# Dense products that read and write backwards, with the high and low parts of a weight side by side

## What is computed

```python
h = rms_norm(x, g_attn_pre[l]) * (1.0 + scale_a[:, None]) + shift_a[:, None]
proj = h @ w_in[l]
...
ff = (jax.nn.silu(h @ w_gate[l]) * (h @ w_up[l])) @ w_down[l]
```

## Time and profile before

| | |
|---|---|
| median of 3 executions | 2589.59 us (2586.76 to 2590.08) |
| the profiled execution | 2586.09 us, of it 2584.3 us span from first to last instruction |
| mean granted clock of TensorE | 0.979 |
| PE busy | 2479.3 us, 96% |
| weight loads (PEld) busy | 2348.3 us, 91% |
| DVE busy | 1439.8 us, 56% |
| ACT busy | 1032.9 us, 40% |
| read from HBM | 498.04 MB, 194 GB/s over the span |

### The profile page before, as it was taken

How to read it: one execution, slowest core, us unless ns; L and a number is a source line. 1 busy time by engine, 2 the same in 40 slices (tenths; PEclk the granted TensorE clock), 3 DMA queues, 4 the chain that set the end, 5 groups by cost and what they waited for, 6 DMA issues and landing times.

```text
span 2584.3 us, 47889 instructions
## 1 busy us (share of the span) xinstructions
PE 2479.3 (96%) x20022; PEld 2348.3 (91%) x20022; DVE 1439.8 (56%) x1926; ACT 1032.9 (40%) x1332; POOL 290.8 (11%) x372
## 2 busy tenths in 40 slices
PE   6999988989999999999989998998999999999999
PEld 4999857979999999999979997878999999999999
DVE  3687657966764444443455554755655555554443
ACT  3533244344333434333334445443444444443333
POOL 5000122410100000011113002113000000000000
PEclk8999989989999999999989999999999999999999
DMA  9887865977785555555544442314455555555553
GB/s 345 290 289 267 292 211 173 334 274 244 249 291 192 186 187 184 184 180 181 189 135 150 148 153 66 115 66 131 148 179 188 181 182 178 179 182 181 190 181 130
DMA packets 263862, 504.24 MB, mean 195 GB/s; under 512 B 17152, under 2 KB 26283, under 8 KB 263467
## 3 DMA queue, kind: packets, MB, share of 16 engines
q1 hardware_dynamic: 257899, 494.97, 57.0%
q10 hardware_dynamic: 5840, 7.52, 0.9%
HBM read 498.04 MB, written 2.10 MB: 194 GB/s over the span
## 4 chain that ended last, share of the span: by engine, by line
PE 80%; DVE 8%; ACT 4%; issue 4%; DMA 2%; SPq 1%; POOL 1%; DVEq 0%; ACTq 0%; POOLq 0%
PE bank L2110 24%; PE bank L2112 24%; PE bank L2111 24%; ACT w_hi L935 3%; DVE w_lo L1458 3%; PE bank L2145 2%; DMA raw<-in_w_in 1%; DVE tmp L1592 1%; DVE ada_acc L1486 1%; DMA staged<-in_w_ada 1%; SPq L646 1%; PE bank L2254 1%; SPq L739 1%; PE bank L2455 0%; ACT x_hi L1046 0%
## 5 line engine op out<-in xcount | busy, mean ns | idle before, releaser
L1458 DVE TENSOR_TENSOR w_lo<-raw,w_hi 128x2048 fp32r<-128x2048 f32 (+3 forms) x386 | 863.5, 2237 | 942.2 <-ACT w_hi L935 941.7
L2110 PE MATMUL bank<-x_hi,w_hi 128*128 128x256 f32 (+2 forms) x4608 | 1317.5, 286 | 35.6 <-DVE w_lo L1458 19.1
L2112 PE MATMUL bank<-x_hi,w_lo 128*128 128x256 f32 (+2 forms) x4608 | 1307.6, 284 | 0.0
L2111 PE MATMUL bank<-x_lo,w_hi 128*128 128x256 f32 (+2 forms) x4608 | 1301.2, 282 | 0.0
L935 ACT ACTIVATE w_hi<-raw 128x2048 fp32r<-128x2048 f32 (+3 forms) x386 | 718.7, 1862 | 1032.8 <-PE bank L2112 905.8
L2110 PEld LDWEIGHTS bank<-x_hi,w_hi 128*128 128x128 f32 x4608 | 873.0, 189 | 71.9 <-issue 40.7
L2111 PEld LDWEIGHTS bank<-x_lo,w_hi 128*128 128x128 f32 x4608 | 873.1, 189 | 1.2 <-issue 1.2
L2112 PEld LDWEIGHTS bank<-x_hi,w_lo 128*128 128x128 f32 x4608 | 872.2, 189 | 0.0
L2112 PE MATMUL bank<-hid_hi,w_lo 128*128 128x256 f32 x1408 | 397.0, 282 | 0.0
L2110 PE MATMUL bank<-hid_hi,w_hi 128*128 128x256 f32 x1408 | 394.1, 280 | 2.8 <-DVE w_lo L1458 1.5
L2111 PE MATMUL bank<-hid_lo,w_hi 128*128 128x256 f32 x1408 | 394.3, 280 | 0.0
(11 more groups left out here) (332 smaller groups left out, 1462.6 us busy)
## 6 DMA issues: line engine op xcount, KB each, us to landing
raw<-in_w_gate SPq DMA_DIRECT2D x88, 1024.0 KB, 5.2
raw<-in_w_up SPq DMA_DIRECT2D x88, 1024.0 KB, 5.2
raw<-in_w_ada SPq DMA_DIRECT2D x72, 1024.0 KB, 6.7
raw<-in_w_in SPq DMA_DIRECT2D x68, 1024.0 KB, 5.7
raw<-in_w_down SPq DMA_DIRECT2D x64, 1024.0 KB, 5.0
raw<-in_w_down SPq DMA_DIRECT2D x32, 768.0 KB, 4.3
beside<-in_w_ada SPq DMA_DIRECT2D x16, 1024.0 KB, 7.5
raw<-in_w_o SPq DMA_DIRECT2D x16, 1024.0 KB, 6.7
```

Of the source, the lines that this page charges most:

```text
L1458: dve.tensor_tensor(w_lo[ps][:, 0:width], raw[slot][:, 0:width], w_hi[ps][:, 0:width], ALU.subtract).then_inc(raw_free[slot], 1)
L2110: pe.matmul(out, wh[:, k, c], hi(k0 + k), start=a0, stop=False)
L2111: pe.matmul(out, wh[:, k, c], lo(k0 + k), start=False, stop=False)
L2112: ins = pe.matmul(out, wl_[:, k, c], hi(k0 + k), start=False, stop=z)
```

## The change

Two edits are made together.

The first is in `dense`: the token operand of each of the three matmuls and the PSUM output are given with the step -1 along the columns. The first column that PE reads is the last one of the row, and it is written to the last column of the output range. Each output column still receives the product of its own token column; results stand where they stood. Weights are still read from the first column to the last.

The second is in the layout of the split weights. In place of four tiles of 2048 columns there are two tiles `w_both` of 2048 by 2 numbers. The high part of a weight is the first 4 bytes of 8, its low part the other 4. The names `w_hi` and `w_lo` stay, as views whose columns lie 8 bytes apart. So ACT writes (L935) with a step of 8 bytes, DVE reads the high part and writes the low part (L1458) with a step of 8 bytes, and the weight loads of all dense matmuls read with that step. The four tiles take the same bytes in all, and everything behind them keeps its address. ACT's two sums of squares at the start (L981), which use `w_hi` as a place for output that nothing reads, write with that step too.

```diff
-        w_hi = [place(f"w_hi{i}", [P, UK * COLS], F32R) for i in range(SPLIT)]
-        w_lo = [place(f"w_lo{i}", [P, UK * COLS], F32R) for i in range(SPLIT)]
+        w_both = [place(f"w_both{i}", [P, UK * COLS, 2], F32R) for i in range(SPLIT)]
+        w_hi, w_lo = ([w[:, :, part] for w in w_both] for part in range(2))
...
-                        out = (banks(m) if banks else bank[base + m])[0:r, 0:n]
+                        out = (banks(m) if banks else bank[base + m])[0:r, 0:n][:, ::-1]
...
-                            pe.matmul(out, wh[:, k, c], hi(k0 + k), start=a0, stop=False)
-                            pe.matmul(out, wh[:, k, c], lo(k0 + k), start=False, stop=False)
-                            ins = pe.matmul(out, wl_[:, k, c], hi(k0 + k), start=False, stop=z)
+                            pe.matmul(out, wh[:, k, c], hi(k0 + k)[:, ::-1], start=a0, stop=False)
+                            pe.matmul(out, wh[:, k, c], lo(k0 + k)[:, ::-1], start=False, stop=False)
+                            ins = pe.matmul(out, wl_[:, k, c], hi(k0 + k)[:, ::-1], start=False, stop=z)
```

## The result

The changed kernel takes 2612.01 us (median of 4 executions, 2607.97 to 2615.33), the kernel before 2588.18 us (4 executions, 2582.34 to 2590.08): 1.0095 times as long, 95% interval 1.0081 to 1.0110, or 24 to 25 us more. The forecast was 2520 us, some 70 us less. The profiled execution took 2615.33 us, at the same mean clock of 0.979.

A forecast was written before the change was run, and what follows sets the result against it. PE's dense matmul steps were taken as the bound. Gains of 79 us, counted as 69 (63% in full, the rest at two thirds), took 2586.1 to 2517; the median's 3.5 us more gave about 2520, range 2470 to 2650.

The forecast's parts named there:

- The gain from streams that keep their distance: Dense matmuls: token reads and weight loads both cover 1024 bytes, so steps fall to 0.113 us with 256 columns; 79 us.
- The floor of 0.112: Lowest step for a dense matmul with 256 columns, in us, read from 128-column weight loads beside one-column matmuls.
- The weight loads with a step of 8 bytes: Dense matmuls' loads of 128 numbers: 6 ns of room, any price over 0.05 ns per number shows; taken as nothing.
- The rival "a few ns": PE's streams: new addresses meet more often, the mean step rises by 3 ns, 54 us, 2640 us; chance 0.10.
- a way to fail: Forecast fails if weight loads have their own rate for stepped reads, with only 6 ns to spare.
- ACT's stepped write: ACT's 2048 numbers per unit, 8 bytes apart: nothing to 0.77 ns per number (1.58 us); taken as nothing.
- the split was to become the bound: Splitting the weights outlasts its slack, from 0.54 ns per number if one engine pays; 2645 to 2985 us, chance 0.15.
- hidden up to the slack: Weight split: extra ACT and DVE time is hidden up to 1.10 us per unit; each us beyond costs half a us.
- DVE's price of nothing: DVE's 8-byte streams in the split: nothing to 1.58 us per unit; taken as nothing.
- Rival 1: Dense matmuls: the 10 to 12 ns are a fixed price of changing weights; 2585 to 2595 us, chance 0.12.
- The 64-column row: Profile row cited against the gain: matmuls with loads of 64 columns look the same as with 128, 300 ns mean.
- a case in which DVE pays for the step and PE gains: DVE pays 0.77 ns per number in the split while PE gains 4 ns a matmul; about 2645 us.

## Why the prediction was wrong

**The gain from streams that keep their distance: the step that failed first.** The sum gives it 79 us, counted as 69, of the 92 us between 2520 and 2612, and it rested on all steps falling to 0.113 us. They did not fall: with both edits the mean is 0.1186 us on `x_hi` and 0.1178 on `hid`, against 0.1173 and 0.1178 before. The direction gives 17 us back where the loads are stepped and takes 3 where they are adjacent, so against the kernel before there is no gain at all. The steps did become even, as expected, but not by the two edits together: backward reads alone do it (0.115 to 0.121 on `hid`, in place of 0.112 to 0.125), with the mean there unchanged and on `x_hi` 0.6 ns higher. Taking the unevenness away took no time away, and the short steps were no evidence of room. The floor of 0.112 was read from loads beside matmuls of one column; single steps with 256 columns come down to it, but no mean comes near. What the remaining 10 ns are made of stays open.

**The weight loads with a step of 8 bytes: taken as nothing.** "Any price over 0.05 ns per number shows at once", it said, and this held. A load of 128 numbers takes 8 ns more, 0.06 ns per number, and the matmul step rises by 0.1193 - 0.1168 = 2.5 ns in the window of the run with stepped loads. That is +31 us alone; with what the backward reads give back, 14 us are left of it in the changed kernel. The rival "a few ns" was the right one, with 3 ns and 54 us for its case and a chance of 0.10, and the end of the prediction names this price as a way to fail.

**ACT's stepped write: mis-sized.** Taken as nothing, it is 0.12 ns per number, 0.24 us per unit, far under the 0.54 from which the split was to become the bound. Yet it costs some 10 us: the rule "hidden up to the slack" was read at one unit, and fails at the places where PE already waits for the split. Rows 4 showed them, 20.6 us of idle time. The trace has 27 such waits; 27 x 0.24 = 6.5 us would have been a fair first estimate, and PE's waits for the split grew by 6.9 us. DVE's price of nothing was right. The Trainium skill's "Vector Engine (DVE) Microarchitecture Reference", section 5.2, which asks for two adjacent words beginning on an 8-byte boundary, does not hold for this step: 2304 ns against 2302, where the estimate from its table was 1.9 us more. The lines of 16 bytes with two hits in each, in the Trainium skill's "SBUF — State Buffer", section "Door 1", fit DVE (nothing at 8 bytes) and roughly the loads (8 ns at 8 bytes, 141 ns at 16), but not ACT's write (237 ns at 8 bytes).

**Rival 1's point that averages lie close** was half right. The 64-column row that spoke for a fixed price compares modelled durations; by start-to-start times in the whole trace the two are close as well, 0.1246 us with 64 columns loaded and 0.1252 with 128, both with 272 moving. But the price is not fixed: on `hid` the mean is 0.1203 us with stepped loads and forward columns, and 0.1200 without the gaps of 64 bytes. The kernel before sits at the best of the three placements tried.

**The range.** That 2612 lies within 2470 to 2650 is luck. The upper end was drawn for a case in which DVE pays for the step and PE gains, and neither happened.

**What was argued only:** that loads run through their columns from the last to the first, so that backward token reads go the same way. No trace here shows the order in which a load reads. It would explain why the direction helps with stepped loads; a load in the other direction was not tried, and what the direction changes at adjacent loads (the evenness) is not explained by it.

## What to carry to other kernels

Where matmuls of 256 columns with a new weight block each start every 0.117 us, a load has no spare time: keep its numbers adjacent, since here a step of 8 bytes cost 2% and one of 16 bytes doubled the time. A delay in a producer that the steady slack hides is still paid where the consumer already waits: count those waits and multiply by the delay before calling it free. Here that gave 5 to 7 us, and the delay cost some 10. Uneven steps are no proof that their mean can fall. The placement of the two streams can matter as much as their pattern (32 bytes were worth 1.6 ns on `x_hi`), so try it by itself.

## What was not expected of the hardware

The direction of a matmul's PSUM writes makes no difference that shows, and that of its moving reads 0.1% (2590.6 and 2590.7 against 2587.8 us) with adjacent weight loads, 0.6% the other way with stepped ones (2599.83 against 2616.72 us). ACT's write with a step of 8 bytes takes 2.07 to 2.09 us per 2048 numbers in the three kernels with forward columns and 2.15 to 2.16 us in the two where PE reads backwards with stepped loads; the cause stays open.
